# The FFN output matrix by the seven-product scheme for 12 of 22 depth tiles, with weight sums made partly by transfers

## The chip, the cores and the metric

One core of a Trainium2 chip runs the kernel. The metric is the device time of one execution in microseconds (us); the time before is the median of three timed runs.

## What is computed

One inference step of a hybrid streaming encoder with two layers, for 512 prompt tokens and 32 sample tokens of width 1024, all in 32-bit floats. Each layer has a SwiGLU feed-forward network (FFN) ahead of its mixer and one behind it, so there are four FFNs of inner width 2816:

```python
def swiglu(h, w_in, w_out):
    gate, up = jnp.split(h @ w_in, 2, axis=-1)
    return (jax.nn.silu(gate) * up) @ w_out

# per layer
x = x + 0.5 * swiglu(rms_norm(x, g1), w_in_a, w_out_a)
x = x + mixer(rms_norm(x, gm))
x = x + 0.5 * swiglu(rms_norm(x, g2), w_in_b, w_out_b)
```

The change touches the four FFNs, above all the product with `w_out` (2816 x 1024, that is 22 depth tiles of 128 by 1024 columns).

## The kernel before

The activations stand with their width on the 128 partitions and the 544 tokens along the free axis, two halves of 272 (`TH`). A product of 32-bit precision is made of three TensorE products: every operand is split into a high part (ScalarE copies it to `float32r`, L778 for weights) and a low part (VectorE subtracts, L784), and high x high, high x low and low x high are summed in PSUM.

An FFN is a list of units (`ffns`). For each of 11 column pairs of 256 columns there is a gate unit and an up unit of the input matrix. The first two pairs are plain (`LEAD_PAIRS`). The other nine go by Strassen's scheme in Winograd's form, here called seven-product: a 256 x 1024 block of weights is taken as 2 x 2 blocks, the tokens as 2 halves, and 7 products of half size take the place of 8 (`ffn_seven_pe`, L892, 7 x 4 x 3 = 84 matmuls of 272 columns). Four of its left factors are sums of weight blocks, which VectorE makes (`weight_sum_dve`, L1038 to L1046, buffers `wsum`), one unit ahead. The token sums stand in `bop`.

The output matrix is plain. Behind each of pairs 2 to 9 stands a `mid` unit (4 depth tiles by 512 columns, 96 matmuls, L793), and four `last` units take the last 6 tiles (72 matmuls each). The hidden rows of a pair are products in `sq`; ScalarE and VectorE split them into `hh` and `hl` (L951, L956).

The order is written out by hand, engine by engine. While TensorE runs product i of a unit, ScalarE and VectorE split product i of the next one, in a ring of 8 entries (`entry`, semaphores `op_hi`, `op_lo`, `op_used`). ScalarE also copies four of the seven products out of PSUM (`m1c`, `m5c`, `u2c`, `u3c`, L1155), and TensorE waits for a copy one product later. SP loads 1 MB of raw weights per unit into two slots (`raw`); a load waits until the unit two before it is split (`raw_free`). POOL has nothing to do in an FFN but its first microseconds and its end.

Of the kernel before, what the change touches and what calls it, by code (L numbers as in the profile page):

```python
# [29 lines left out]
P = 128  # L30
# [17 lines left out]
MID_TILES = 4  # L48
MID_PARTS = 4
LAST_TILES = FT - MID_TILES * MID_PARTS  # L50
RING = 8
# [104 lines left out]
def build(nc, ctx, io):  # L156
# [84 lines left out]
    ffn = Overlay(nc, arena.at, top)  # L241
    hh = ffn.buf("hh", [P, KT, T], F32R)
    hl = ffn.buf("hl", [P, KT, T], F32R)
# [5 lines left out]
    half_tiles = (KT // 2) * T * 4  # L249
    wsum_at = [Overlay(nc, arena.at + half_tiles, top), Overlay(nc, arena.at + 3 * half_tiles, top)]  # L250
    wsum_first = [w.buf(f"wsum_first{i}", [P, 4, KH, P]) for i, w in enumerate(wsum_at)]
    sum_at = Overlay(nc, norm_at.at, norm_end)
    wsum = [sum_at.buf(f"wsum{i}", [P, 4, KH, P]) for i in range(2)]
    comb_at = Overlay(nc, norm_at.at + KT * T * 4, norm_end)
    m1c, m5c, u2c, u3c = ([comb_at.buf(f"{name}{i}", [P, TH]) for i in range(2)] for name in ("m1c", "m5c", "u2c", "u3c"))
# [150 lines left out]
    sum_made = sig("sum_made")  # L406
    bank_copied = sig("bank_copied")
# [32 lines left out]
    comb = sig("comb")  # L440
# [106 lines left out]
    sm_tables = sig("sm_tables")  # L547
# [21 lines left out]
    def raw_index(u):  # L569

        return u + (0 if u < 1 else 33 if u < 20 else 66 if u < 21 else 99)
# [9 lines left out]
    sevens = []  # L581
    for f in range(4):
        units = []
        add = lambda kind, pair, s=0, part=0: units.append(Unit(f, len(units), kind, pair, s, part))
        for j in range(FJ):
            for s in range(2):
                add("whole" if j == 0 and s == 0 else "plain" if j < LEAD_PAIRS else "seven", j, s)
            if LEAD_PAIRS <= j < LEAD_PAIRS + 2 * MID_PARTS:
                add("mid", (j - LEAD_PAIRS) % 2, 0, (j - LEAD_PAIRS) // 2)
        for q in range(4):  # L590
            add("last", q, q % 2, MID_PARTS)
        ring_pos = (ring_pos + RING - 1) // RING * RING + KH
        for u in units:
            u.op = op_count
            u.n_ops = {"whole": 0, "plain": 4, "seven": 7, "mid": 4, "last": 4}[u.kind]
            if u.kind == "last":
                ring_pos += -ring_pos % 4
            if u.kind == "seven":
                u.seven = len(sevens)
                sevens.append(u)  # L600
            for i in range(u.n_ops):
                e = ring_pos % RING
                op_entry.append(e)
# [13 lines left out]
    first_seven = [u[2 * LEAD_PAIRS].seven for u in ffns]  # L617
    by_raw = {u.raw: u for units in ffns for u in units}
# [149 lines left out]
    def op_split_hi(act, u, i):  # L768
# [3 lines left out]
        if u.kind == "seven" and i in S_SUMS:  # L772
            act.wait_ge(sum_made.sem, sum_made.at(4 * u.seven + S_SUMS[i] + 1))
# [4 lines left out]
        nc.scalar.activation(entry(op)[0][:, 0:block_nk(u, i), :], op_source(u, i), ACT.Copy).then_inc(op_hi.sem, 1)  # L778
# [2826 lines left out]
```

## Time and profile before

| | us |
|---|---|
| timed runs, median (lowest, highest) | 2288.67 (2287.71, 2289.91) |
| profiled execution: its span from first to last instruction | 2285.9 |
| TensorE busy in it | 2249.8 (98%) |
| VectorE busy | 1633.5 (71%) |
| ScalarE busy | 1049.8 (46%) |
| POOL busy | 302.4 (13%) |

The profiled execution's own time is its span and the little that lies before its first and behind its last instruction; the timed runs are 1.8 to 4.0 us longer than the span. Shares of busy time are averages over the whole span. The granted clock of TensorE was 0.996 of 2.4 GHz in the mean.

### The profile page before, as it was taken

Reading aid. Unit: us, or ns where it says so; the run is one execution under the profiler, and the core shown is the slowest. Engines: PE = TensorE matmul, PEld = TensorE weight load, DVE = VectorE, ACT = ScalarE, POOL = GpSimd, SP = SyncE. Lnnn points to the kernel's source line nnn. Section 1 sums busy time; section 2 is a strip of 40 time slices with the busy share of each in tenths; the row PEclk is TensorE's granted clock in tenths of the full one; section 3 lists DMA queues with packets and bytes.
Section 4 is the critical chain, followed back from the end, with each engine's and each line's share of the span. In section 5 each row is a group of like instructions: output and inputs, shape, how many; then the busy total and the mean of one; then the engine's idle time right before and its main releaser. Section 6 shows DMA issues by size and latency. Waiting matters only on the chain.

```text
span 2285.9 us, 45730 instructions
## 1 busy us (share of the span) xinstructions
PE 2249.8 (98%) x18915; PEld 2198.7 (96%) x18915; DVE 1633.5 (71%) x2712; ACT 1049.8 (46%) x1949; POOL 302.4 (13%) x257
## 2 busy tenths in 40 slices
PE   9999999999999999999999999999999999999998
PEld 8999999988989999999999999999988899999998
DVE  7876776557575977767877776689755657777674
ACT  5544444333323544444554444454444544444443
POOL 2100002000051100001200000144033632000001
PEclk9999999999999999999999999999999999999999
DMA  4222323322202233222222232322310012222321
GB/s 135 93 93 97 103 92 110 98 81 83 90 10 93 75 101 103 93 93 93 93 93 93 96 105 87 114 74 75 93 52 2 30 31 91 93 93 93 98 97 68
DMA packets 175052, 194.82 MB, mean 85 GB/s; under 512 B 4826, under 2 KB 155870, under 8 KB 174841
## 3 DMA queue, kind: packets, MB, share of 16 engines
q1 hardware_dynamic: 161902, 181.64, 24.3%
q10 hardware_dynamic: 12306, 8.18, 1.3%
q8 instruction: 151, 2.47, 0.5%
q0 software_dynamic: 640, 2.10, 0.3%
q14 instruction: 53, 0.43, 0.1%
HBM read 185.80 MB, written 6.10 MB: 84 GB/s over the span
## 4 chain that ended last, share of the span: by engine, by line
PE 85%; DVE 8%; ACT 2%; issue 2%; POOL 1%; DMA 1%; ACTq 0%; SPq 0%; DVEq 0%; POOLq 0%
PE ps L892 33%; PE ps L793 29%; PE ps L666 12%; DVE cacc L2419 2%; DVE wl L651 1%; PE ps L3320 1%; DVE pre L2408 1%; ACT cacc L2488 1%; DMA xnat<-x_prompt 1%; PE ps L1681 1%; PE ps L3165 0%; POOL dBl L2996 0%; PE ps L2152 0%; PE ps L3150 0%; PE ps L3200 0%
## 5 line engine op out<-in xcount | busy, mean ns | idle before, releaser
L892 PE MATMUL ps<-bop,wh 128*128 128x272 f32 x4032 | 761.0, 288 | 0.0
L892 PEld LDWEIGHTS ps<-bop,wh 128*128 128x128 f32 x4032 | 633.0, 188 | 0.0
L892 PE MATMUL ps<-bop,wl 128*128 128x272 f32 x2016 | 582.2, 289 | 0.0
L784 DVE TENSOR_TENSOR wl<-raw,wh 128x512 fp32r<-128x512 f32 (+1 forms) x456 | 317.5, 708 | 266.8 <-ACT wh L778 262.1
L892 PEld LDWEIGHTS ps<-bop,wl 128*128 128x128 f32 x2016 | 378.8, 188 | 0.0
L778 ACT ACTIVATE wh<-raw 128x512 fp32r<-128x512 f32 (+1 forms) x456 | 265.3, 611 | 217.2 <-PE ps L793 177.4
L793 PE MATMUL ps<-hl,wh 128*128 128x288 f32 (+1 forms) x1408 | 290.4, 287 | 0.0
L793 PE MATMUL ps<-hh,wl 128*128 128x288 f32 (+1 forms) x1408 | 289.5, 287 | 0.0
L793 PE MATMUL ps<-hh,wh 128*128 128x288 f32 (+1 forms) x1408 | 289.1, 286 | 0.0
L666 PE MATMUL ps<-xh,wh 128*128 128x288 f32 (+1 forms) x1056 | 224.7, 294 | 2.1 <-DVE wl L651 2.1
L778 ACT ACTIVATE wh<-wsum 128x512 fp32r<-128x512 f32 x256 | 159.6, 627 | 132.8 <-DVE wsum L1038 86.6
L666 PE MATMUL ps<-xl,wh 128*128 128x288 f32 (+1 forms) x1056 | 217.9, 287 | 0.0
L666 PE MATMUL ps<-xh,wl 128*128 128x288 f32 (+1 forms) x1056 | 217.3, 287 | 0.0
L793 PEld LDWEIGHTS ps<-hh,wh 128*128 128x128 f32 x1408 | 215.8, 188 | 0.0
L793 PEld LDWEIGHTS ps<-hh,wl 128*128 128x128 f32 x1408 | 215.3, 188 | 0.0
L793 PEld LDWEIGHTS ps<-hl,wh 128*128 128x128 f32 x1408 | 215.0, 188 | 0.0
L784 DVE TENSOR_TENSOR wl<-wsum,wh 128x512 fp32r<-128x512 f32 x256 | 175.3, 686 | 17.4 <-ACT wh L778 14.0
L699 POOL COPY ssq<-sq 128x544 f32<-128x544 f32 x7 | 5.7, 810 | 1270.6 <-ACT sq L685 1270.6
L666 PEld LDWEIGHTS ps<-xh,wh 128*128 128x128 f32 x1056 | 161.6, 188 | 11.8 <-issue 7.4
L666 PEld LDWEIGHTS ps<-xl,wh 128*128 128x128 f32 x1056 | 161.5, 188 | 0.0
L666 PEld LDWEIGHTS ps<-xh,wl 128*128 128x128 f32 x1056 | 161.5, 188 | 0.0
L651 DVE TENSOR_TENSOR wl<-raw,wh 128x2048 fp32r<-128x2048 f32 x41 | 94.1, 2294 | 31.2 <-ACT wh L646 31.2
(490 smaller groups left out, 3586.5 us busy)
## 6 DMA issues: line engine op xcount, KB each, us to landing
raw<-ffn_w_in SPq DMA_DIRECT2D x88, 1024.0 KB, 5.0
raw<-ffn_w_out SPq DMA_DIRECT2D x32, 1024.0 KB, 5.1
raw<-odd_w_in SPq DMA_DIRECT2D x16, 1024.0 KB, 5.7
raw<-even_w_in SPq DMA_DIRECT2D x14, 1024.0 KB, 5.0
raw<-ffn_w_out SPq DMA_DIRECT2D x16, 768.0 KB, 4.2
raw<-even_w_out SPq DMA_DIRECT2D x4, 1024.0 KB, 5.0
raw<-odd_w_out SPq DMA_DIRECT2D x4, 1024.0 KB, 4.9
xnat<-x_prompt SPq DMA_DIRECT2D x2, 1024.0 KB, 11.9
```

Source lines behind the costliest of these rows:

```text
L651: nc.vector.tensor_tensor(wl[slot][:, 0:kt, :], raw[slot][:, 0:kt, :], wh[slot][:, 0:kt, :].bitcast(F32), ALU.subtract).then_inc(lo_done.s ...
L666: ins = nc.tensor.matmul(ps[:, 2 * pe_out + b, PCOLS[b]], w, r[:, rk, TOKENS[b]], start=first and a == 0, stop=last and a == 2)
L699: nc.gpsimd.tensor_copy(ssq[:], sq[0][:]).then_inc(ssq_done.sem, 1)
L778: nc.scalar.activation(entry(op)[0][:, 0:block_nk(u, i), :], op_source(u, i), ACT.Copy).then_inc(op_hi.sem, 1)
L784: nc.vector.tensor_tensor(lo[:, 0:nk, :], op_source(u, i), hi[:, 0:nk, :].bitcast(F32), ALU.subtract).then_inc(op_lo.sem, 1)
L793: ins = nc.tensor.matmul(ps[:, 2 * pe_out + b, PCOLS[b]], w[:, k, :], r[:, rk + k, TOKENS[b]], start=first and k == 0 and a == 0, stop=las ...
L892: ins = nc.tensor.matmul(ps[:, bank, 0:TH], w[:, k, :], bop[:, r, k, :], start=i in S_OPEN and k == 0 and a == 0, stop=k == KH - 1 and a = ...
L1681: ins = nc.tensor.matmul(ps[:, 4 + m, 0:width(b)], att[64 * m:64 * m + 64, h, b * P:(b + 1) * P], att[64 * m:64 * m + 64, 4 + h, 0:width(b ...
L2408: nc.vector.tensor_tensor(pre[c][:, 3:3 + SEQ], flat[:, PAT:PAT + SEQ], rstd[:, 0:SEQ], ALU.mult)
L2419: nc.vector.scalar_tensor_tensor(out=cacc[c][:], in0=pre[c][:, r:r + PADT - 3], scalar=cols[:, 7 * KT + 7 * i + r:7 * KT + 7 * i + r + 1], ...
L2488: nc.scalar.activation(cacc[i % 2][:], pre[i % 2][:, 0:PADT - 3], ACT.Copy, scale=cols[:, 7 * KT + 7 * i:7 * KT + 7 * i + 1]).then_inc(tap ...
L3320: ins = nc.tensor.matmul(ps[:, 2 * (2 * q + c) + b, OUT_COLS[b]], w, r[:, k, OUT_TOKENS[b]], start=k == 0 and a == 0, stop=k == KT - 1 and ...
```

## The change

Depth tiles 6 to 17 of the output matrix, two thirds (`part` 1 and 2) of 6 tiles each, go by the seven-product scheme: for each third four `out` units of 256 columns, 7 products of 3 tiles, 63 matmuls. Tiles 0 to 5 (`part` 0) stay plain, in four `mid` units of 72 matmuls, and tiles 18 to 21 in two `last` units of 96. The four units of a third stand between the gate and the up unit of pair 3, 6 and 9.

The right factors of the new products are the hidden rows. For pairs 3 to 8 VectorE makes four token differences of them (`hidden_turns`, into `hopf`), ScalarE and VectorE split seven blocks into `hop`, all in the gate unit of the next pair. Signs are turned so that all weight sums are additions (`minus`, `scale=-1.0`).

The two sums that are made of raw blocks alone (numbers 0 and 3) are no longer made by VectorE, other than in the first two input units of an FFN: POOL loads one block from DRAM into the buffer, waits, and adds the other with an accumulating transfer (`ffn_sums_pool`). Sums 1 and 2 stay with VectorE. The outcome of an `out` unit goes into `x` in five steps (`x_add`, `tail_dve`).

```diff
-MID_TILES = 4
-MID_PARTS = 4
+MID_PAIRS = 3
+MID_TILES = 2 * MID_PAIRS
+MID_PARTS = 3
...
         for j in range(FJ):
...
+            add("whole" if j == 0 else kind, j, 0)
+            if j and j % MID_PAIRS == 0:
+                for q in range(4):
+                    add("mid" if j == MID_PAIRS else "out", q, 0, j // MID_PAIRS - 1)
+            add(kind, j, 1)
+        for q in range(2):
+            add("last", q)
...
+    def sum_wait(eng, u, k):
+        if not early_block(u) and k in (0, 3):
+            eng.wait_ge(sum_added.sem, sum_added.at(32 * late_before(u) + 32))
...
+    def ffn_out_pe(pe, u):
...
+        for i, o in enumerate(S_ORDER):
...
+            elif i in (1, 5) and not first:
+                pe.wait_ge(x_part.sem, x_part.at(x_steps(u, 4) - X_STEPS))
+            elif i in (2, 3, 4):
+                pe.wait_ge(bank_copied.sem, bank_copied.at(4 * u.block + i - 1))
...
+            for k in range(MID_PAIRS):
+                for a, (w, r) in enumerate(((w_hi, 7 + o), (w_hi, o), (w_lo, 7 + o))):
+                    ins = nc.tensor.matmul(ps[:, block_bank(u, i), 0:TH], w[:, k, :], hop[k][:, r, :],
...
+    def hidden_turns(dve, u):
...
+        nc.vector.tensor_tensor(f[:, 3, :], sq[0][:, 0:TH], sq[0][:, TH:T], ALU.subtract).then_inc(turn_made.sem, 1)
+        nc.vector.scalar_tensor_tensor(out=f[:, 1, :], in0=sq[1][:, TH:T], scalar=-1.0, in1=sq[0][:, TH:T],
+                                       op0=ALU.mult, op1=ALU.subtract).then_inc(turn_made.sem, 1)
+        dve.wait_ge(turn_made.sem, turn_made.at(turns_before(u) + 1))
+        nc.vector.tensor_tensor(f[:, 2, :], sq[1][:, TH:T], f[:, 3, :], ALU.subtract).then_inc(turn_made.sem, 1)
+        dve.wait_ge(turn_made.sem, turn_made.at(turns_before(u) + 3))
+        nc.vector.tensor_tensor(f[:, 0, :], sq[1][:, 0:TH], f[:, 2, :], ALU.subtract).then_inc(turn_made.sem, 1)
...
+    def ffn_sums_pool(pool, f, w_in, w_out):
...
+        for u in ffns[f]:
+            if u.n_ops != 7 or early_block(u):
+                continue
+            out = sums_of(u)
+            if u.block - first_block[f] < 4:
+                pool.wait_ge(op_used.sem, op_used.at(ffns[f][3].op + 4))
+            else:
+                pool.wait_ge(op_lo.sem, op_lo.at(blocks[u.block - 2].op + 5))
+            pool.dma_start(out[:, 0, :, :], block(u, 1, 0)).then_inc(sum_loaded.sem, 16)
+            pool.dma_start(out[:, 3, :, :], block(u, 0, 0)).then_inc(sum_loaded.sem, 16)
+            pool.wait_ge(sum_loaded.sem, sum_loaded.at(32 * late_before(u) + 32))
+            pool.dma_start(out[:, 0, :, :], block(u, 1, 1), accum_op=ALU.add).then_inc(sum_added.sem, 16)
+            pool.dma_start(out[:, 3, :, :], block(u, 1, 0), accum_op=ALU.add).then_inc(sum_added.sem, 16)
...
+    def ffn_out_dve(dve, u):
+        v = ffns[u.f][u.at + 1]
+        weight_sum_dve(dve, v, 1)
+        next_split(dve, op_split_lo, u, 0)
+        tail_dve(dve, ffns[u.f][u.at - 1])
+        weight_sum_dve(dve, v, 2)
+        next_split(dve, op_split_lo, u, 1)
+        next_split(dve, op_split_lo, u, 2)
+        x_add(dve, u, 1)
+        next_split(dve, op_split_lo, u, 3)
+        x_add(dve, u, 2)
...
```

How it changes the order, at three places. In these rows a name behind the operation is output <- inputs, with its size, and in brackets the semaphores that the instruction waits for.

POOL in the first FFN, before: the gates of the lead, and then the sums of squares at the FFN's end.

```order
L1024 TENSOR_TENSOR gbuf_68<-gbuf_68,rstd 128x544 [waits gate_silu]
L1024 TENSOR_TENSOR gbuf_69<-gbuf_69,rstd 128x544 [waits gate_silu]
L699 COPY ssq<-sq 128x544 [waits sq_ready]
L703 TENSOR_TENSOR ssq<-ssq,sq 128x544 [waits sq_ready,ssq_done] x7
L1483 MEMSET qdec 128x64
```

POOL at the same place after (two blocks of the 24 of an FFN):

```order
L1185 TENSOR_TENSOR gbuf_69<-gbuf_69,rstd 128x544 [waits gate_silu]
L1229 DMA wsum_73<-ffn_w_in 128x4x128 [waits op_used]
L1230 DMA wsum_73<-ffn_w_in 128x4x128
L1232 DMA wsum_73<-ffn_w_in 128x4x128 [waits sum_loaded]
L1233 DMA wsum_73<-ffn_w_in 128x4x128
L1229 DMA wsum_72<-ffn_w_in 128x4x128 [waits op_lo]
L1230 DMA wsum_72<-ffn_w_in 128x4x128
L1232 DMA wsum_72<-ffn_w_in 128x4x128 [waits sum_loaded]
L1233 DMA wsum_72<-ffn_w_in 128x4x128
```

Four transfers per block stand there now, the third behind a wait for the landing of the first two.

VectorE just behind an up unit, before: the tail product, then sums and splits for the next unit, and the low parts of the hidden rows (`hl`) in a plain unit.

```order
L1206 TENSOR_TENSOR sq<-ps,gbuf_69 128x272 [waits block_silu,op_used]
L1038 TENSOR_TENSOR wsum_72<-raw 128x512 [waits raw_loaded1]
L784 TENSOR_TENSOR wl_50<-raw,wh_49 128x512 [waits op_hi]
L1041 TENSOR_TENSOR wsum_72<-wsum_72,raw 128x512 [waits sum_made]
L784 TENSOR_TENSOR wl_50<-wsum_72,wh_49 128x512 [waits op_hi]
L1216 SCALAR_TENSOR_TENSOR x<-ps,x 128x544 [waits x_part,op_used]
L1044 TENSOR_TENSOR wsum_72<-raw,wsum_72 128x512 [waits sum_made]
L1046 TENSOR_TENSOR wsum_72<-raw 128x512
L956 TENSOR_TENSOR hl<-sq,hh 128x544 [waits hh_ready]
```

VectorE at the same place after, in a gate unit:

```order
L1204 TENSOR_TENSOR wsum_73<-wsum_73,raw 128x512 [waits raw_loaded1,sum_added]
L1419 TENSOR_TENSOR sq<-ps,gbuf_69 128x272 [waits block_silu,op_used]
L1093 TENSOR_TENSOR hopf_79<-sq 128x272 [waits h_made]
L1094 SCALAR_TENSOR_TENSOR hopf_79<-sq 128x272
L1097 TENSOR_TENSOR hopf_79<-sq,hopf_79 128x272 [waits turn_made]
L1099 TENSOR_TENSOR hopf_79<-sq,hopf_79 128x272 [waits turn_made]
L824 TENSOR_TENSOR wl<-wsum_73,wh 128x512 [waits op_hi]
L1117 TENSOR_TENSOR hop_80<-sq,hop_80 128x272 [waits hh_ready]
L1207 TENSOR_TENSOR wsum_73<-raw,wsum_73 128x512 [waits sum_made]
L824 TENSOR_TENSOR wl<-wsum_73,wh 128x512 [waits op_hi]
L1114 SCALAR_TENSOR_TENSOR hop_80<-sq,hop_80 128x544 [waits hh_ready]
```

The first of them waits for POOL's transfers (`sum_added`); two of the four sums are gone, and the token differences and three low parts stand among the splits.

VectorE in an `out` unit, which was not there before:

```order
L1204 TENSOR_TENSOR wsum_73<-wsum_73,raw 128x384 [waits raw_loaded1,sum_added]
L824 TENSOR_TENSOR wl_50<-raw,wh_49 128x384 [waits op_hi]
L1424 SCALAR_TENSOR_TENSOR x<-ps,x 128x272 [waits x_part,op_used]
L1207 TENSOR_TENSOR wsum_73<-raw,wsum_73 128x384 [waits sum_made]
L824 TENSOR_TENSOR wl_50<-wsum_73,wh_49 128x384 [waits op_hi] x2
L1444 TENSOR_TENSOR x<-x,comb_74 128x272 [waits x_part,bank_copied]
L824 TENSOR_TENSOR wl<-wsum_73,wh 128x384 [waits op_hi]
L1448 TENSOR_TENSOR x<-x,comb_74 128x544 [waits x_part,bank_copied]
```

Here the splits are 384 columns wide, and the steps into `x` stand between them.

## Rows read from the trace of the kernel before

**Rows 1.** The page, busy time and the chain that ended last, by engine.

```profile
span 2285.9 us, 45730 instructions
PE 2249.8 (98%) x18915; PEld 2198.7 (96%) x18915; DVE 1633.5 (71%) x2712; ACT 1049.8 (46%) x1949; POOL 302.4 (13%) x257
...
PE 85%; DVE 8%; ACT 2%; issue 2%; POOL 1%; DMA 1%; ACTq 0%; SPq 0%; DVEq 0%; POOLq 0%
```

**Rows 2.** The chain in order of time, first FFN: start us, us, what.

```profile
106.14 21.12 PE ps L892 x168
127.26 12.01 PE ps L793 x96
139.27 21.11 PE ps L892 x168
160.38 11.96 PE ps L793 x96
...
193.44 11.91 PE ps L793 x96
...
337.62 21.09 PE ps L892 x168
358.71 35.87 PE ps L793 x288
394.58 6.02 PE ps L666 x48
```

**Rows 3.** Busy time by stage, first FFN; the last two columns are DMA share and GB/s.

```profile
core 0: us, PE busy (x) PEld busy (x) DVE busy (x) ACT busy (x) POOL busy (x), PEclk, DMA share, GB/s
94.16:106.14 11.98, 11.98 (x99) 11.98 (x98) 11.98 (x22) 4.65 (x8) 0.00 (x0) 1.00 0.28 89
127.26:139.27 12.01, 12.01 (x99) 12.01 (x98) 11.33 (x19) 4.76 (x8) 0.00 (x0) 1.00 0.29 91
139.27:160.38 21.11, 21.11 (x171) 21.11 (x170) 12.58 (x23) 10.91 (x23) 0.00 (x0) 1.00 0.29 100
```

**Rows 4.** VectorE in order of time: start us, us, line, operation, tiles, sizes.

```profile
58.94 1.27 DVE L972 TENSOR_TENSOR bop<-bopf,bop 128x1088 fp32r<-128x1088 f32 x1
60.14 0.67 DVE L1041 TENSOR_TENSOR wsum_first<-wsum_first,raw 128x512 f32<-128x512 f32 x1
...
127.13 0.72 DVE L1259 TENSOR_TENSOR sq<-sq,gbuf 128x544 f32<-128x544 f32 x1
127.77 0.43 DVE L1206 TENSOR_TENSOR sq<-ps,gbuf 128x272 f32<-128x272 f32 x1
128.12 0.68 DVE L1038 TENSOR_TENSOR wsum<-raw 128x512 f32<-128x512 f32 x1
128.72 0.69 DVE L784 TENSOR_TENSOR wl<-raw,wh 128x512 fp32r<-128x512 f32 x1
...
146.08 0.69 DVE L784 TENSOR_TENSOR wl<-wsum,wh 128x512 fp32r<-128x512 f32 x1 [0.21 <-ACT wh L778]
...
149.02 0.69 DVE L784 TENSOR_TENSOR wl<-raw,wh 128x512 fp32r<-128x512 f32 x1 [0.18 <-ACT wh L778]
```

**Rows 5.** ScalarE in order of time, in an up unit.

```profile
154.39 0.40 ACT L1155 ACTIVATE u2c<-ps 128x272 f32<-128x272 f32 x1 [1.11 <-PE ps L892]
154.68 0.62 ACT L778 ACTIVATE wh<-raw 128x512 fp32r<-128x512 f32 x1
...
157.71 1.67 ACT L778 ACTIVATE wh<-raw 128x512 fp32r<-128x512 f32 x3
```

**Rows 6.** Transfers in 139.27:160.38, then 440:450, then 466:474: packets, MB, share of 16 engines.

```profile
q1 hardware_dynamic: 1560, 2.08, 28.4%
...
raw<-ffn_w_in SPq DMA_DIRECT2D x1, 1024.0 KB, 4.8
...
q10 hardware_dynamic: 676, 0.32, 15.5%
q0 software_dynamic: 80, 0.26, 7.5%
...
q0 software_dynamic: 80, 0.26, 12.3%
```

**Rows 7.** POOL's loads of 256 KB, tiles pks and pvs: issue ns, landing us.

```profile
L1487 POOL DMA_DIRECT2D pks<-cache_attn_k x4: 747/748/919, 398.4 to 515.7; - x4
DMA to landing us min/median/max: 3.8/5.5/6.5
...
L1490 POOL DMA_DIRECT2D pvs<-cache_attn_v x4: 747/748/757, 399.4 to 544.1; - x4
...
DMA to landing us min/median/max: 3.2/3.5/3.9
```

**Rows 8.** SP's issues of raw loads in order of time.

```profile
138.02 0.37 SPq L1447 DMA_DIRECT2D raw<-ffn_w_out  x1
149.74 11.02 SPq L1447 DMA_DIRECT2D raw<-ffn_w_in  x2
```

**Rows 9.** A group of instructions by line: POOL's sums of squares (busy us, mean ns).

```profile
L703 POOL TENSOR_TENSOR ssq<-ssq,sq 128x544 f32<-128x544 f32 x49 | 70.5, 1439 | 125.1 <-ACT sq L685 123.6 <-POOL ssq L703 1.1 <-POOL ssq L699 0.4
```

More of the change, by code:

```diff
@@ L585, in build @@
         for j in range(FJ):
[L586 to L591, printed above, removed]
+            kind = "plain" if j < LEAD_PAIRS else "seven"
+            add("whole" if j == 0 else kind, j, 0)
[5 more added lines that the diff above has]
+            add("last", q)
         ring_pos = (ring_pos + RING - 1) // RING * RING + KH
@@ L594, in build @@
             u.op = op_count
-            u.n_ops = {"whole": 0, "plain": 4, "seven": 7, "mid": 4, "last": 4}[u.kind]
+            u.n_ops = {"whole": 0, "plain": 4, "seven": 7, "out": 7, "mid": 4, "last": 4}[u.kind]
             if u.kind == "last":
-                ring_pos += -ring_pos % 4
+                ring_pos += -ring_pos % (RING if u.pair == 0 else 4)
             if u.kind == "seven":
@@ L600, in build @@
                 sevens.append(u)
+            if u.kind == "out":
+                u.out = len(outs)
+                outs.append(u)
+            if u.n_ops == 7:
+                u.block = len(blocks)
+                blocks.append(u)
             for i in range(u.n_ops):
                 e = ring_pos % RING
+                if u.kind == "last" and u.pair == 0:
+                    e = (i + 2) % 4
                 op_entry.append(e)
@@ new lines, in x_steps, with x_before, hidden_before @@
+    def x_steps(u, step):
+        if u.kind == "mid":
+            return X_LAYER * u.f + 2 * u.pair + step
+        return X_LAYER * u.f + 8 + X_STEPS * (4 * (u.part - 1) + u.pair) + step
+    def x_before(u, step):
+        if u.part == 1:
+            return X_LAYER * u.f + 2 * u.pair + 2
+        return x_steps(u, step) - 4 * X_STEPS
+    def hidden_before(f, pair):
+        whole = MID_PAIRS * MID_PARTS
+        done = lambda j: 2 * j + min(max(j - MID_PAIRS, 0), whole - MID_PAIRS)
+        return f * done(FJ) + done(pair)
@@ L1187, in ffn_last_act @@
             split_hi(act, next_unit, 0)
-        for c in range(2):
-            feed_act(act, n, 2 * u.pair + c, c, not final)
+        for c in range(4):
+            feed_act(act, n, 4 * u.pair + c, c % 2, not final)
     def ffn_act(act, f, n, next_unit=None):
@@ L1311, in ffn_last_dve @@
                 feed_dve(dve, n, m)
+        if q == 0:
+            tail_dve(dve, before)
+            op_split_lo(dve, u, 2)
+            op_split_lo(dve, u, 3)
+            hidden_lo(dve, before, 0)
+            hidden_lo(dve, before, 1)
+            for i in range(4):
+                op_split_lo(dve, ffns[f][u.at + 1], i)
+        for m in range(4 * q, 4 * q + 4):
+            update(m)
+            if m == 4 and next_unit is not None:
+                split_lo(dve, next_unit, 0)
+            if m:
+                feed(m - 1)
+        if q:
+            feed(KT - 1)
     def ffn_dve(dve, f, n, next_unit=None):
```

533 lines of the change are left out of this document (339 added, 194 removed).

## The prediction

> **What bounds the kernel now.** I read the chain that ended last, first by engine [rows 1]: TensorE holds 85% of it, VectorE 8%. Then the same chain in order of time through the first FFN [rows 2]. The reader is to see that each piece begins where the one before ended: 106.14 + 21.12 is 127.26, 127.26 + 12.01 is 139.27, and so on to 394.58. A piece of L892 with 168 matmuls is a pair of seven-product units, a piece of L793 with 96 a plain unit of the output matrix, the one with 288 the four last units. No wait stands between them, and the other three FFNs look the same. Third, busy time by stage [rows 3]: TensorE is full everywhere, VectorE has 12.58 us of work in the 21.11 us of a pair and 11.33 in the 12.01 of a plain output unit, the DMA engines are 0.29 busy. So in an FFN a matmul less is a matmul's time less, as long as VectorE, ScalarE and the transfers keep up. What the change is worth is first a count of matmuls and then a question to those three.
>
> **TensorE.** A pair of units takes 21.09 to 21.12 us for 168 matmuls [rows 2], 0.1256 us each. The eight plain units of an FFN take 11.91 to 12.01 [rows 2], 11.97 in the mean, 0.1247 per matmul; the 288 of the last units 35.87, 0.1245. Before, the output matrix of one FFN has 8 x 96 + 288 = 1056 matmuls: 95.7 + 35.9 = 131.6 us. After: four plain units of 72 (6 tiles, 2 column halves, 3 products, 2 token halves), 288 x 0.1247 = 35.9; eight seven-product units of 63 (7 products, 3 tiles, 3), 504 x 0.1256 = 63.3; two last units of 96, 192 x 0.1245 = 23.9; sum 123.1. That is 8.5 us less per FFN and **34 us less** in four. The 18 seven-product input units of an FFN, 84 matmuls each, are not touched.
>
> **VectorE.** Its instructions overlap at their ends, so I count starts [rows 4]: 0.60 us for 512 columns (128.12 to 128.72), 0.64 for 544, 0.35 for 272, 1.20 for 1088 (58.94 to 60.14); 384 columns, interpolated, 0.47. In a gate unit behind an up unit of pairs 3 to 8 it now has 7 low parts (4.2), 2 weight sums (1.2), the tail product (0.35), 4 token differences (1.4), low parts of 272, 544 and 1088 columns (2.2) and 3 sums (1.05): 10.4 of 10.55 us. The up unit has 4.2 + 1.2 + 5 small ones 2.0 = 7.4. An output unit of 7.91 has 7 x 0.47 + 2 x 0.47 + 3 x 0.35 + 2 x 0.64 = 6.6; the fourth, which splits for a 512-column unit, 7.7. Three pairs and four output units make 79.9 us of 95.0, 84%, where it was 72% [rows 3]. Before, VectorE was busy 11.98 of 11.98 us in the first plain unit and TensorE did not wait [rows 3]: the splits run seven products ahead, so a lag of a microsecond in the gate unit is caught up in the up unit. I cost VectorE at nothing. If that cover fails, below. ScalarE has 7 splits, 4 copies and the new high parts, 7 x 0.56 + 4 x 0.30 + 1.9 = 7.0 of 10.55 in the gate unit [rows 5]; its copy has to be done one product (1.51 us, in output units 1.13) after it may start and takes 0.40, so it too has cover.
>
> **Transfers.** Of the four sums of 64 input units and all 32 output units, two leave VectorE: per block POOL now issues two loads of 256 KB, waits for both, issues two accumulating ones, and ScalarE waits for these before it splits product 1. In a 21.11 us pair the two raw loads hold the 16 engines for 28.4%, 6.0 us, so 3.0 per MB [rows 6]. A 256 KB load from POOL in the same 512-byte pieces held them 12.3% of 8 us, 0.98, or 7.5% of 10 us, 0.75 [rows 6]. No row shows an accumulating transfer. A gain is excluded, since it moves what a load moves and reads its destination too; so its lower end is 0.75. The dearest 512-byte row is the ScalarE queue's stores, 15.5% of 10 us for 0.32 MB [rows 6], 1.27 for 256 KB; read twice that is 2.5, my upper end. I take 1.6, two quiet loads, nearer the lower end since the sizes and the queue are those of the POOL rows. A unit then needs 3.0 + 2 x 0.98 + 2 x 1.6 = 8.2 of its 10.55 us of engine time (10.0 at the upper end), an output unit three quarters of that, 6.1 (7.5) of 7.91. So it fits at both ends, narrowly at the upper one.
>
> The Trainium skill, in "Collectives: The Full Stack", section "The bandwidth ceiling: the fold count and why AG ≠ RS ≠ AR", says that an add in the transfer costs no cycles of its own but two source reads, so that a reducing transfer ran at half the rate of a copy. No run here shows that yet; by it an accumulate is two of the 0.98, an estimate of 2.0 us, and the unit needs 9.0 of 10.55, the same verdict.
>
> **The wait that is added.** What counts is also how long the four transfers take one behind the other. POOL issues in 0.75 us, a load lands 3.2 to 6.5 us after its issue [rows 7]. Two steps of issue and landing are 7.9 us at the quick end, 14.5 at the slow one, plus at most 2 x (2.5 - 0.75) = 3.5 for the adding. The buffer comes free when VectorE has the fifth low part of the block before last, 7.5 us into a unit (146.08 + 0.69 - 139.27 [rows 4]) or, in the fuller gate unit, about 9.7. The sums are wanted about 3.3 us into the unit after next, since ScalarE must split product 1 and copy the second product before TensorE's fourth at 4.5. That leaves 14.7 us (0.85 + 10.55 + 3.3) or 16.6 for input units; for output units and the one or two behind them 1.7 + 7.9 + 2.4 = 12.0. Queued behind a late sum are ScalarE's copies, for which TensorE waits, and VectorE's next sum. I take landings of 3.8 and 1.7 for the adding: 10.8 us, which is 4 us early in input units and 1 us early at the ends of the output groups. With some late ones there, I put 2 us on the whole kernel (eight groups, a quarter of a microsecond each). At the slow end, 18 against 14.7 and 12.0 and halved because two blocks are in flight, it would be 106 us for the 64 input units alone.
>
> **Raw loads.** The next load starts when the seventh low part is done (149.02 + 0.69; SP issues at 149.74 [rows 4, 8]) and takes 4.8 [rows 6]. It now shares the engines with 5.2 us of the POOL queue's work in the same unit: 10.0 at worst, of 9.4 to 10.7 and some 2 us until TensorE's third product feels it. Nothing, or half a microsecond in some units. I add 0.5 us in all.
>
> **Ends of the FFNs.** The chunks of 1/8 of the output now end every 24 matmuls, 3.0 us, instead of 36. What follows each of them, VectorE's update (0.64) and low part, ScalarE's high part and square and POOL's sum of squares at 1.44 [rows 9], is under 3 us on each engine, and POOL's last weight sum is issued more than a unit before. I cost it at nothing; a microsecond either way per FFN lies inside the range.
>
> **Sum.** The profiled execution has a span of 2285.9 us; the three timed runs stand 1.8 to 4.0 above it, the median 2.8. 2285.9 - 34 + 2.5 = 2254.4 of span, with 2.8 around it **2257**.
>
> **Rivals.**
> (a) **The accumulating transfers are slow** and the transfers become the bound, by engine time or, with landings at the slow end, by the chain above. It decides where 3.0 + 1.96 + 2A passes 10.55, at A = 2.8 us per 256 KB. At A = 3.5 a unit needs 12.0 and an output unit 9.0: 64 x 1.4 + 32 x 1.1 = 125 us, less 34 and more 2.8 around: 2285.9 + 91 + 2.8 = 2380, slower. For it: 512-byte pieces, two thirds of the engine time already spoken for, no row of its own kind, two landings in series with the slowest seen at 6.5 [rows 7]. Against: the POOL queue's pieces are the cheapest per byte in the trace [rows 6].
> (b) **VectorE becomes the bound** in the gate units. The last two token differences each wait for the one before, as do other pairs; at 0.2 us for five such waits the gate unit has 11.4 us for 10.55. If the up unit doesn't give it back, 24 gate units cost 0.85 each, 20 us: 2275, still faster. Against it speak the full VectorE of the first plain unit [rows 3] and 3 us of room in each up unit.
> (c) **Most of it is given back** by late sums around the output groups and raw loads that land late in them: 1 us in each of 32 output units gives 2287, no difference.
>
> **How the numbers follow.** My forecast, 2251 to 2265: 0.58. (b) or a part of (c), 2265 to 2284: 0.13. (c) in full, 2284 to 2293: 0.06. (a): 0.23, spread from 2293 up with a long tail, since each half microsecond of A past its point costs 64 x 1.0 + 32 x 0.75 = 88 us. A measurement of this kernel can tell 0.2%, 4.6 us, from no change: faster 0.71, same 0.06, slower 0.23. The first three cases hold 0.77; with the near end of (a) up to 2300 the range 2250 to 2300 holds 0.8.
>
> **What would show it.** In the profile after, the chain in time should show output groups of 252 matmuls in about 31.7 us and last units of 192 in 23.9, and 288 matmuls fewer. Right: TensorE full in every FFN stage, sums landing before ScalarE wants them, VectorE near 84%. Wrong by (a): ScalarE's splits of wsum waiting for DMA, pairs longer than 21.1 us, the DMA share near 1. Wrong by (b): VectorE full in gate units and TensorE waiting for wl. Wrong by (c): waits in and just behind output groups alone.

## The result, and the profile after

The changed kernel takes 2360.42 us (median of 4 runs, 2357.14 to 2370.72) against 2288.19 us: **3.2% slower**, a ratio of 1.032 with an interval of 1.031 to 1.034. The forecast was 2257 us, faster. The profiled execution has a span of 2354.9 us, 69.0 more than before.

The page of the kernel after, busy time, the transfer queues (packets, MB, share of 16 engines) and the chain by engine and line, to be read against [rows 1]:

```profile
span 2354.9 us, 46614 instructions
PE 2245.2 (95%) x18627; PEld 2187.7 (93%) x18627; DVE 1705.3 (72%) x2960; ACT 1166.3 (50%) x2229; POOL 707.5 (30%) x641
...
q0 software_dynamic: 108160, 94.40, 23.0%
...
PE 65%; DMA 15%; DVE 9%; POOL 5%; issue 4%; ACT 2%; ACTq 0%; SPq 0%; DVEq 0%; POOLq 0%
```

The 288 matmuls are gone (18915 to 18627). But TensorE holds 65% of the chain instead of 85%, and transfers and POOL, 2% together before, now hold 20%.

The chain in order of time through the first output group, to be read against [rows 2], where no wait stood between the pieces:

```profile
106.28 36.07 PE ps L1000 x288
142.35 52.79 PE ps L932 x420
...
203.99 0.77 POOL wsum L1229
204.75 4.84 DMA wsum<-ffn_w_out
209.89 1.29 POOL wsum L1232
211.18 1.32 POOL wsum L1233
212.50 0.62 POOL wsum L1229
213.11 5.99 DMA wsum<-ffn_w_out
219.40 1.29 POOL wsum L1232
220.68 1.31 POOL wsum L1233
221.99 0.79 POOL wsum L1229
222.78 2.87 issue
225.65 6.59 DMA wsum<-ffn_w_in
232.53 0.77 POOL wsum L1232
233.31 7.47 DMA wsum<-ffn_w_in
241.86 6.06 PE ps L979 x36
```

The plain output units take 36.07 us, as costed, and five units of 84 matmuls follow without a gap. From 203.99 to 240.78 the path runs through POOL and its transfers alone: two loads (L1229, L1230), their landing, two adding issues (L1232, L1233), and only then the loads of the next block. (240.78 is 233.31 + 7.47, where the last landing ends.) What the chain releases is in ScalarE's order of time (what ended the idle time stands in brackets):

```profile
232.44 0.38 ACT L1356 ACTIVATE comb<-ps 128x272 f32<-128x272 f32 x1
240.80 0.63 ACT L818 ACTIVATE wh<-wsum 128x512 fp32r<-128x512 f32 x1 [7.99 <-DMA wsum<-ffn_w_in]
241.34 0.38 ACT L1356 ACTIVATE comb<-ps 128x272 f32<-128x272 f32 x1
```

ScalarE stands 7.99 us in front of a late sum, and behind it in ScalarE's order is a copy of a product (`comb`) that TensorE waits for. So a late sum of the *next* unit stops TensorE in *this* one. Over the whole span (us, times, longest):

```profile
DVE wsum L1204 <- DMA wsum<-ffn_w_in: 72.7, 23, 9.3
ACT wh L818 <- DMA wsum<-ffn_w_in: 65.9, 22, 8.7
DVE wsum L1204 <- DMA wsum<-ffn_w_out: 59.6, 20, 7.4
PE ps L979 <- ACT comb L1356: 55.6, 15, 7.9
```

By place, in windows of the first FFN (the columns of [rows 3]; an output group is 252 matmuls):

```profile
142.18:205.50 63.32, 63.32 (x507) 63.32 (x505) 55.78 (x104) 40.12 (x81) 24.93 (x24) 1.00 0.81 182
205.50:247.76 42.26, 33.62 (x255) 33.05 (x253) 26.66 (x54) 20.84 (x47) 16.18 (x17) 0.92 0.76 173
247.76:312.58 64.82, 63.77 (x506) 63.39 (x505) 55.49 (x104) 40.01 (x81) 24.64 (x24) 1.00 0.79 180
312.58:353.58 41.00, 34.18 (x254) 33.80 (x253) 27.37 (x56) 20.96 (x47) 14.38 (x16) 0.92 0.72 168
353.58:393.36 39.78, 33.18 (x255) 32.99 (x253) 20.89 (x39) 17.18 (x35) 5.83 (x6) 0.91 0.50 119
```

A group takes 41 to 42 us here (38.8 to 44.4 in all four FFNs) where the prediction said 31.7. Of the first group's 10.7 us too many, 8.6 are idle time; in the other 2.1 TensorE is busy for 33.62 us with what takes 31.54 at full clock, at a granted clock of 0.92 of 2.4 GHz in the mean of that stretch. The mean is made of two levels. TensorE stood idle from 234.5 to 241.86 us, and around the end of that wait the clock is 0.50, that is 1.2 GHz:

```profile
237.95:244.78 6.83, 2.92 (x13) 2.95 (x14) 3.98 (x8) 2.79 (x6) 2.15 (x2) 0.50 0.58 121
```

The 36 matmuls behind the wait take 6.06 us (last row of the chain above), 1.6 more than 36 take in 31.54 us for 252. In the full stretches the clock is 1.00.

### The profile page after: what moved, and what is told of

Read it like the earlier page. It is cut to its first block, busy times and chain, and to the rows that moved or that the text cites. A ratio compares the mean times of both kernels' runs of the same rounds, so it can differ in the third digit from the quotient of the medians.

```text
span 2354.9 us, 46614 instructions
## 1 busy us (share of the span) xinstructions
PE 2245.2 (95%) x18627; PEld 2187.7 (93%) x18627; DVE 1705.3 (72%) x2960; ACT 1166.3 (50%) x2229; POOL 707.5 (30%) x641
## 3 DMA queue, kind: packets, MB, share of 16 engines
q0 software_dynamic: 108160, 94.40, 23.0%
## 4 chain that ended last, share of the span: by engine, by line
PE 65%; DMA 15%; DVE 9%; POOL 5%; issue 4%; ACT 2%; ACTq 0%; SPq 0%; DVEq 0%; POOLq 0%
PE ps L932 22%; PE ps L688 15%; DMA wsum<-ffn_w_in 9%; PE ps L833 8%; PE ps L1000 6%; DMA wsum<-ffn_w_out 5%; PE ps L1034 2%; POOL wsum L1232 2%; PE ps L979 1%; POOL wsum L1233 1%; PE ps L3577 1%; DVE wl L673 1%; DVE cacc L2676 1%; POOL wsum L1229 1%; DVE wl L824 1%
## 5 line engine op out<-in xcount | busy, mean ns | idle before, releaser
L824 DVE TENSOR_TENSOR wl<-raw,wh 128x512 fp32r<-128x512 f32 (+1 forms) x456 | 291.9, 657 | 57.5 <-ACT wh L818 52.7
L979 PE MATMUL ps<-hop,wh 128*128 128x272 f32 x1344 | 269.7, 300 | 55.9 <-ACT comb L1356 55.6
L818 ACT ACTIVATE wh<-wsum 128x512 fp32r<-128x512 f32 (+1 forms) x384 | 226.4, 590 | 183.8 <-DMA wsum<-ffn_w_in 65.9
L824 DVE TENSOR_TENSOR wl<-wsum,wh 128x512 fp32r<-128x512 f32 (+1 forms) x384 | 243.8, 642 | 49.4 <-ACT wh L818 47.7
L979 PEld LDWEIGHTS ps<-hop,wh 128*128 128x128 f32 x1344 | 223.0, 199 | 59.8 <-issue 59.7
L1356 ACT ACTIVATE comb<-ps 128x272 f32<-128x272 f32 x416 | 163.8, 394 | 187.3 <-PE ps L932 146.9
L979 PE MATMUL ps<-hop,wl 128*128 128x272 f32 x672 | 199.9, 297 | 0.0
L1232 POOL DMA_DIRECT2D wsum<-ffn_w_in x64 | 83.8, 1310 | 306.4 <-DMA wsum<-ffn_w_in 306.4
L688 PEld LDWEIGHTS ps<-xh,wh 128*128 128x128 f32 x1056 | 162.2, 189 | 12.7 <-issue 7.9
L1204 DVE TENSOR_TENSOR wsum<-wsum,raw 128x512 f32<-128x512 f32 (+1 forms) x96 | 61.8, 643 | 132.7 <-DMA wsum<-ffn_w_in 72.7
L1229 POOL DMA_DIRECT2D wsum<-ffn_w_in x64 | 72.1, 1127 | 247.4 <-DVE wl L824 219.5
L979 PEld LDWEIGHTS ps<-hop,wl 128*128 128x128 f32 x672 | 133.5, 199 | 0.0
```

Of the source, the lines that this page charges most:

```text
L688: ins = nc.tensor.matmul(ps[:, 2 * pe_out + b, PCOLS[b]], w, r[:, rk, TOKENS[b]], start=first and a == 0, stop=last and a == 2)
L818: nc.scalar.activation(entry(op)[0][:, 0:block_nk(u), :], op_source(u, i), ACT.Copy).then_inc(op_hi.sem, 1)
L824: nc.vector.tensor_tensor(lo[:, 0:nk, :], op_source(u, i), hi[:, 0:nk, :].bitcast(F32), ALU.subtract).then_inc(op_lo.sem, 1)
L979: ins = nc.tensor.matmul(ps[:, block_bank(u, i), 0:TH], w[:, k, :], hop[k][:, r, :], start=i in S_OPEN and k == 0 and a == 0, stop=k == MI ...
L1204: nc.vector.tensor_tensor(out[:, 1, :, :], out[:, 0, :, :], block_raw(u, 0, 0), ALU.add).then_inc(sum_made.sem, 1)
L1229: pool.dma_start(out[:, 0, :, :], block(u, 1, 0)).then_inc(sum_loaded.sem, 16)
```

## Experiments

All times are medians beside runs of the kernel before on the same chip (2288.3 to 2288.8 us). Stage times come from each kernel's own trace. Two words are used throughout: the *chain* of a block is the time from the issue of its first load to the landing of its last adding transfer, and its *window* the time from that first load to ScalarE's first split of a sum of that block, when nothing is late.

### Which blocks lose: half of them by transfers

in_only leaves transfers to the 64 input blocks, out_only to the 32 output blocks; VectorE makes the other sums, as it does in early blocks.

```diff
+    def by_dma(u):
+        return not early_block(u) and u.kind != "out"     # out_only: == "out"
...
-            if u.n_ops != 7 or early_block(u):
+            if u.n_ops != 7 or not by_dma(u):
```

> Output units make all four weight sums on VectorE again; only the 64 input blocks keep POOL's transfers. Theory 1 (the late sums come from POOL's serial chain, which takes 8.4 to 8.7 us and more per block from one first load to the next where an output unit has 7.91, so it falls behind inside the output groups and delivers late until behind them): the 75.7 us that the eight output groups lose go, with most of the 22 us in the input units between and behind them; groups of 252 matmuls near 31.7 us, 2265 to 2280 in all. Theory 2 (the engines' time for the adding is the limit): the input blocks still move 1 MB by transfers per unit, so pairs of input units keep losing; 2290 to 2320. Theory 3 (VectorE is too full): its work per output unit rises from about 6.6 to 7.5 of 7.91 us, the groups stay above 34 us; over 2300.

> The converse: all input units make their four sums on VectorE, only the 32 output blocks go by transfers. Theory 1 in the form of occupancy and backlog: POOL comes to each group idle and the first two blocks' sums are early; it then falls behind by 0.5 to 0.8 us per block, so a group loses 1 to 3 us instead of 10; about 2275 to 2290. Theory 1 in the form of latency (12.3 us of chain against a window of 12.0, whatever stands ahead): the groups still lose 5 us or more each; 2300 to 2340. Theory 3: gate units hold about 11.6 us of VectorE work in 10.55; pairs rise above 21.2 us each, 20 us more in 24 pairs.

in_only: 2318.43 us, ratio 1.0135 (1.012 to 1.015). The groups come down to 31.5 to 33.7 us, but the input units between and behind them now lose: their three-pair stretches behind a group take 65.0 to 71.5 us instead of 63.3, the last stretch of three units of each FFN 33.4 to 43.1 instead of 31.7. The 2265 to 2280 of theory 1 was wrong: the blocks right behind a group are as exposed as those in it. The time lies in the range of theory 2 (2290 to 2320), so the places have to decide. Three windows of its first FFN, ahead of the first group, behind it and behind the second:

```profile
141.44:204.75 63.31, 63.31 (x506) 63.31 (x505) 55.77 (x104) 40.26 (x81) 15.17 (x14) 1.00 0.67 157
236.99:301.99 65.00, 63.79 (x507) 63.41 (x506) 57.44 (x108) 40.28 (x81) 16.76 (x16) 1.00 0.68 159
333.50:373.72 40.22, 34.04 (x254) 33.65 (x253) 21.73 (x41) 17.17 (x35) 4.65 (x5) 0.92 0.50 118
```

Ahead of a group every unit moves its 1 MB too, at the same share of the engines (0.67), and nothing is lost; by theory 2 it should be. out_only: 2314.35 (four runs from 2303 to 2320), ratio 1.011 (1.008 to 1.014); nearly all its loss lies in the groups, 36.2 to 41.9 us each. That is the latency form of theory 1; the idle queue at the group's start did not help. Theory 3 fails in both: in_only's groups stay below 34 us, and in out_only VectorE's fuller units run at 63.5 us per three pairs.

### No transfers, and transfers that don't add

dve_all is the same edit with `by_dma` always false. no_add keeps every wait:

```diff
-            pool.dma_start(out[:, 0, :, :], block(u, 1, 1), accum_op=ALU.add).then_inc(sum_added.sem, 16)
-            pool.dma_start(out[:, 3, :, :], block(u, 1, 0), accum_op=ALU.add).then_inc(sum_added.sem, 16)
+            pool.dma_start(out[:, 0, :, :], block(u, 1, 1)).then_inc(sum_added.sem, 16)
+            pool.dma_start(out[:, 3, :, :], block(u, 1, 0)).then_inc(sum_added.sem, 16)
```

> No sum goes by transfers: VectorE makes all four in every seven-product unit, the new output units included. VectorE then has about 20.2 of 21.1 us in a pair with hidden splits and 7.5 of 7.91 in an output unit. Theory 1 and 2: all of the loss goes, the matmul count alone is left, 2255 to 2265. Theory 3 (VectorE becomes the bound when it is 95% full): 2275 to 2300, with TensorE waiting for wl in the gate units.

> The two accumulating transfers of each block become plain loads of the same blocks to the same place, with the same waits (the blocks' sums 0 and 3 are then not added up, and the outcome is wrong by that part). It takes the adding away and leaves the chain of two issues and two landings. If the adding itself is the cost (2.08 against some 0.98 us of engine time for 256 KB, and issues of 1.3 and 1.9 us against 0.8): the groups fall to about 32 us and the kernel to 2265 or less. If two landings in series on one queue are the cost: per block the chain gets shorter by about 1.5 us of issue and some landing, 11 against 12.3 us, the groups stay at 34 to 38 us and the kernel at 2290 to 2330.

dve_all: **2258.56 us**, ratio 0.987 (0.985 to 0.989), faster than both kernels. Three pairs and a group of it:

```profile
141.45:204.98 63.53, 63.53 (x507) 63.42 (x506) 60.42 (x113) 40.67 (x81) 0.00 (x0) 1.00 0.28 92
204.98:236.52 31.54, 31.54 (x255) 31.54 (x253) 30.86 (x63) 20.98 (x47) 0.00 (x0) 1.00 0.36 118
```

VectorE is busy 95% and 98% of these stretches and TensorE does not wait: the room that the transfers were to make was not needed. no_add: 2258.75, ratio 0.987 (0.986 to 0.989). The same chain of two issues, a landing, two issues and a landing, over the same bytes, costs next to nothing when the second pair is plain. The queue on its page, and POOL's two second issues in input units among the groups by line (busy us, mean ns of one):

```profile
q0 software_dynamic: 29312, 94.40, 14.2%
...
L1233 POOL DMA_DIRECT2D wsum<-ffn_w_in x64 | 47.9, 748 | 0.5 <-issue 0.5
L1232 POOL DMA_DIRECT2D wsum<-ffn_w_in x64 | 47.9, 748 | 232.9 <-DMA wsum<-ffn_w_in 224.9 <-issue 8.0
```

The same two groups in the changed kernel:

```profile
L1233 POOL DMA_DIRECT2D wsum<-ffn_w_in x64 | 118.7, 1855 | 0.0
L1232 POOL DMA_DIRECT2D wsum<-ffn_w_in x64 | 83.8, 1310 | 306.4 <-DMA wsum<-ffn_w_in 306.4
```

The adding ones take 1.31 and 1.86 us instead of 0.75 each; they overlap, and POOL is free 2.6 us after the start of the first (209.89 to 212.50 in the chain above) instead of 1.5. From issue of the first load to the last landing a block takes, in the median, 9.0 us (output) and 10.9 us (input) in no_add, 12.3 and 13.4 in the changed kernel.

### Half a dose, and the same dose issued late

one_sum leaves only sum 0 to transfers: one load and one adding transfer per block.

```diff
-        elif k == 3 and early:
+        elif k == 3:
...
-            pool.dma_start(out[:, 3, :, :], block(u, 0, 0)).then_inc(sum_loaded.sem, 16)
...
-            pool.dma_start(out[:, 3, :, :], block(u, 1, 0), accum_op=ALU.add).then_inc(sum_added.sem, 16)
```

one_late is one_sum with the load of a block issued later.

```diff
-                pool.wait_ge(op_lo.sem, op_lo.at(blocks[u.block - 2].op + 5))
+                pool.wait_ge(op_lo.sem, op_lo.at(blocks[u.block - 1].op + 2))
```

Theory A in the expectations from here on is that loads standing in POOL's one queue behind the adding transfers of the block before make the next block late; theory B, that the adding itself costs, wherever the loads stand.

> Half a dose: per block only sum 0 goes by transfers (one load, one accumulating), sum 3 is made by VectorE. POOL's work per block falls from about 8.5 to 6 us (0.78 + 3.5 + 1.3), the chain from 12.3 to about 9 us (one landing of 3.5, one of 4.3, issues). Theory A and the reading by chain and window both expect no late sums: 2258 to 2265. Theory B by engine time halves the loss: 2300. If VectorE's third sum costs anything, dve_all with four sums has already shown that it does not.

> one_sum (one load and one accumulating transfer per block), but issued later: when VectorE has the second low part of the block directly before, instead of the fifth of the block before last, 4.5 us later in output units and some 6 us later in input units. The same transfers, the same engine time, less than half of the accumulating ones of the changed kernel. By chain and window the blocks then stand one behind the other: a unit lasts at least the chain plus about 1.5 us of splits, 8.0 + 1.5 = 9.5 against 7.91 in output units and 9.4 + 1.5 = 10.9 against 10.55 in input units; 32 x 1.6 + 64 x 0.4 = 77 us, about 2330. By engine time or slow adding as such: no change from one_sum, 2255 to 2260.

one_sum: **2255.19 us**, ratio 0.986 (0.984 to 0.987), the lowest median here, though its interval overlaps that of dve_all. Its chain in order of time is what the prediction had drawn:

```profile
104.89 36.07 PE ps L1000 x288
140.97 63.32 PE ps L932 x504
204.28 31.54 PE ps L979 x252
235.82 63.31 PE ps L932 x504
299.13 31.51 PE ps L979 x252
```

Without stalls its trace also shows the real window: 12.8 to 15.2 us in steady input units, 12.7 to 14.4 in the first two output units, but 10.5 us in the third and fourth output unit and 10.9 to 11.4 in the two blocks behind them. ScalarE is there a little before TensorE needs it (in sp_loads2, below, a wait of 2.1 us there left TensorE idle for 1.4). The chains of one_sum (8.0 us output, 9.4 input) fit.

one_late: 2458.11, ratio 1.074 (1.073 to 1.076), with the same transfers. POOL in the first group:

```profile
211.62 0.77 POOL L1229 DMA_DIRECT2D wsum<-ffn_w_out  x1 [5.74 <-DVE wl L824]
215.04 1.28 POOL L1231 DMA_DIRECT2D wsum<-ffn_w_out  x1 [2.64 <-DMA wsum<-ffn_w_out]
224.74 0.77 POOL L1229 DMA_DIRECT2D wsum<-ffn_w_out  x1 [8.43 <-DVE wl L824]
```

The blocks stand one behind the other, 13.1 us from load to load where a unit has 7.91, and groups take 47 to 51 us. That latency against a window decides, at a light load on the transfer engines, is shown. The size was off (about 2330 expected): the chain grew to 10 us in the group, and from landing to VectorE's second low part it is 3.1 us, not 1.5.

### The same work, issued earlier or on another queue

early_load changes one wait: slot 0 of the buffer is loaded three products earlier.

```diff
-                pool.wait_ge(op_lo.sem, op_lo.at(blocks[u.block - 2].op + 5))
+                pool.wait_ge(op_lo.sem, op_lo.at(blocks[u.block - 2].op + 2))
             pool.dma_start(out[:, 0, :, :], block(u, 1, 0)).then_inc(sum_loaded.sem, 16)
+            if u.block - first_block[f] >= 4:
+                pool.wait_ge(op_lo.sem, op_lo.at(blocks[u.block - 2].op + 5))
```

> The changed kernel with the same four transfers per block, but the load of sum 0 no longer waits for the whole buffer: it is issued when VectorE has the second low part of the block before last (slot 0 of the buffer is not read after that), three products earlier; the load of sum 3 keeps its wait. Nothing is taken away, so a theory that the adding costs engine time or slows other transfers expects no change, 2350 to 2365. The theory that the sums come late because two loads, two landings and two adding issues stand in series after the buffer is free expects from the load of sum 3 on 0.8 + 3.3 + 6.2 = 10.3 us in output blocks and about 11 in input blocks, where the copy without stalls (one_sum) leaves 10.5 us in the third and fourth output unit and 11.0 to 11.4 in the two blocks behind: most of the 100 us of stalls goes, 2262 to 2285.

2314.68 us, ratio 1.012 (1.010 to 1.014): 46 us better than the changed kernel, 30 short of what was expected. Five of its eight groups take 31.8 to 32.8 us, among them both of the third FFN, in windows:

```profile
1298.86:1331.19 32.33, 31.78 (x255) 31.59 (x253) 26.10 (x52) 20.87 (x47) 15.93 (x15) 1.00 0.90 214
...
1395.56:1427.88 32.32, 31.75 (x254) 31.56 (x253) 26.07 (x52) 20.92 (x47) 15.91 (x15) 1.00 0.91 213
```

The changed kernel's two groups in that FFN:

```profile
1321.60:1360.40 38.80, 34.22 (x254) 33.93 (x253) 25.63 (x52) 20.91 (x47) 15.15 (x15) 0.91 0.80 183
1424.26:1468.70 44.44, 34.41 (x254) 33.85 (x253) 27.16 (x55) 20.84 (x47) 16.99 (x17) 0.88 0.73 168
```

With the same transfers the engines are busy 0.90 of the time and TensorE loses 0.8 us per group; in the changed kernel they are busy 0.73 to 0.80 and it loses 7 to 13. So the engines' time is not what stops it. The other three groups, the first ones of FFNs 1, 2 and 4 (39.8 to 41.5 us), and the last seven-product units of FFNs 1, 2 and 4 (36.3 to 40.3, where one_sum has 31.7) hold most of what is left. At just those places POOL stands still between two issues. The changed kernel's POOL at the first of them, in order of time:

```profile
220.16 1.83 POOL L1233 DMA_DIRECT2D wsum<-ffn_w_out  x1
221.06 1.72 POOL L1229 DMA_DIRECT2D wsum<-ffn_w_in  x1
225.65 0.77 POOL L1230 DMA_DIRECT2D wsum<-ffn_w_in  x1 [2.87 <-issue]
```

It has nine such stalls, 32.6 us of idle time, always at the second load of the 12th, 17th and 23rd of an FFN's 24 blocks (none in the third FFN), and each ends 0.25 us after the last adding transfer of the block before has landed. Where that one has landed in time, as always in one_sum, there is none. In early_load the same issues of the same FFNs go out 0.25 us after the landing.

sp_loads gives the two plain loads to SP's hardware queue, and sp_loads2 places the first two blocks' loads better.

```diff
-            pool.dma_start(out[:, 0, :, :], block(u, 1, 0)).then_inc(sum_loaded.sem, 16)
-            pool.dma_start(out[:, 3, :, :], block(u, 0, 0)).then_inc(sum_loaded.sem, 16)
             pool.wait_ge(sum_loaded.sem, sum_loaded.at(32 * late_before(u) + 32))
+            pool.wait_ge(sum_added.sem, sum_added.at(32 * late_before(u)))
...
+        sp.dma_start(out[:, 0, :, :], sum_block(u, 1, 0, wi, wo)).then_inc(sum_loaded.sem, 16)
+        sp.dma_start(out[:, 3, :, :], sum_block(u, 0, 0, wi, wo)).then_inc(sum_loaded.sem, 16)
```

> The two plain loads of each block are issued by SP on its hardware queue (ahead of the raw load of the same unit, behind the same wait for the buffer), POOL is left with the wait for them and the two accumulating transfers (behind the landing of the block before). The adding stays as dear as it is. Theory A (queue: what costs is that loads stand in POOL's one queue behind the accumulating transfers of the block before, land after 5.5 to 9 us instead of 3.5, and make the next block late in turn): loads land in about 3.5 to 4.5 us, the chain falls from 12.3 to about 10.5 us in output blocks, the groups to 32 to 33 us, 2262 to 2275 in all. Theory B (the adding itself, by its engine time and its 3.2 us of issue and 4.3 to 6 us of landing, wherever the loads stand): the groups still lose 3 to 8 us each, 2290 to 2330. SP also waits for buffers now, with the raw loads queued behind it: if that is late, TensorE waits for raw in up units.

> As sp_loads, but the loads of the first two late blocks of an FFN stand together behind the raw load of the first of them; in sp_loads the second pair stood behind the raw loads of the plain output units and came 40 us late, so that the plain output units took 41 to 42 us instead of 36.1. Expected by chain and window: these 20 us go; the output blocks (10.2 us of chain) are in time, the first input block behind a group (13.7 us of chain against 11.0) stays late by 2 to 3 us; 2290 to 2300. If the loads' place on POOL's queue were the whole cause: 2262 to 2275.

sp_loads: 2322.81 (ratio 1.014), in the range of theory B; sp_loads2: 2307.47 (1.008, 1.005 to 1.010), 7 us above what was expected. In sp_loads2 the output blocks' chain is 10.1 us and the groups take 32.4 to 35.9 us, so that all eight lose 16.6 us together where the changed kernel loses 76.8; ScalarE still waits about 2 us for the input blocks behind them, whose chain is 13 to 16 us against the 11. The first three seven-product units of each FFN take 36.7 to 38.9 us instead of 31.6, a loss that the expectation did not have: the first block's loads are issued at 76.3 us instead of 73.6 and its adding transfers take up to 8.3 us to land. So loads that stand in line behind adding transfers are a good part of the groups' loss, and not the whole cause: with the loads on another queue the chain of the input blocks behind a group is still longer than their window.

### The sums on POOL itself

In pool_add the four transfers of a block go, and POOL adds out of the raw slots:

```diff
+            nc.gpsimd.tensor_tensor(out[:, 0, :, :], block_raw(u, 1, 0), block_raw(u, 1, 1), ALU.add).then_inc(sum_added.sem, 1)
+            nc.gpsimd.tensor_tensor(out[:, 3, :, :], block_raw(u, 0, 0), block_raw(u, 1, 0), ALU.add).then_inc(sum_added.sem, 1)
```

> POOL makes sums 0 and 3 itself, by two additions of 512 or 384 columns out of the raw slots, with the same wait for the buffer and one for the raw load; no transfers for sums. By POOL's rows (1.38 us for 512 columns) that is 2.8 us of POOL per unit of 10.55 and 2.1 per output unit of 7.91, and the raw block lands a unit ahead, so sums come early. If engines do not disturb each other: as dve_all or 1 to 2 us less, 2255 to 2259. If POOL's additions slow VectorE's instructions (both read the same buffers): VectorE's splits of 512 columns rise from 0.69 us, 2260 to 2275.

2294.86 us, ratio 1.003 (1.002 to 1.004), 20 us above the dearer of the two expectations. VectorE's splits of sums, 686 ns in one_sum, take 801, and three pairs of units (second row, a window) last 66.02 us with VectorE busy 62.19 of them:

```profile
L824 DVE TENSOR_TENSOR wl<-wsum,wh 128x512 fp32r<-128x512 f32 x256 | 203.7, 801 | 17.2 <-ACT wh L818 14.2
...
141.34:207.36 66.02, 64.48 (x507) 63.55 (x505) 62.19 (x98) 39.78 (x81) 17.57 (x12) 1.00 0.27 89
```

The transfers are gone, and VectorE is slower while POOL adds: of those 256 splits the 183 that no addition of POOL overlaps take 0.68 us in the mean, the 39 that lie beside one for over four fifths of their length 1.36. ScalarE waits 58.7 us in all for the sum of L1207, 30.0 at the same place of dve_all. That VectorE is the bound here is read from these rows; VectorE was as busy in dve_all (95%) without holding anything up, and no further run tested it.

## Why the prediction was wrong

**TensorE: right.** Plain units 36.07 us for 288 matmuls (35.9 costed), groups 31.5 (31.7), last units 23.9 (23.9). Where nothing stalls, in one_sum, the span is 2253.0, 32.9 below before; 34 were costed, and 2254.4 was the span forecast.

**VectorE at nothing: right,** with more to spare than I claimed. Three pairs and a group were costed at 79.9 us of 95.0, 84% (the terms add up to 80.9); they hold 82.4 in the changed kernel (55.78 and 26.66 in the windows above), and in dve_all VectorE is busy 95% without harm. Rival (b) did not decide; pool_add is the run nearest to it.

**Transfers by engine time: right in the verdict, wrong in a reason.** The queue's share of 16 engines rose from 14.2% of 2255.1 us in no_add to 23.0% of 2354.9 for the same 94.40 MB: 221 us more, for 46.1 MB of adding transfers, 1.26 us per 256 KB. A plain one there is 0.89 (313 us, without 7 for the other loads, for 92.3 MB), so an adding one is 2.15, inside my 0.75 to 2.5 but above the 1.6 taken. I put it near the low end because "the sizes" were those of the POOL rows. They were not: 80 packets for 0.26 MB stand in [rows 6], 3.3 KB each, and the adding transfers bring 78,848 more packets, as 46.1 MB in pieces of 512 bytes do against 4 KB. The Trainium skill ("Collectives: The Full Stack", section "The bandwidth ceiling: the fold count and why AG ≠ RS ≠ AR") says a reducing transfer reads two sources and runs at half a copy's rate; here it is 2.4 times a copy's engine time, and the measurement stands. Neither figure decides the result. (In rival (a) "two thirds of the engine time already spoken for" is under a half by the prediction's own terms, 3.0 + 1.96 of 10.55 us.)

**"The wait that is added" is the step that failed:** 2 us on the whole kernel, 101.9 measured (2354.9 less 2253.0): 76.8 in the eight groups, 24.5 in seven-product input units. Three of its numbers were off. The chain was taken as 10.8 us and is 12.3 in output and 13.4 in input blocks in the median, up to 20.8. Issue was taken as 0.75 us; adding ones take 1.31 and 1.86, and the second load of a block starts 0.8 us after the first and lands about 1 us later still. And the windows, 12.0 and 14.7 by my sum, are 10.5 to 11.4 and 12.8 to 15.2 in one_sum. (The 16.6 beside them is 16.9 by its own terms, and was not used.)

**What I left out** is that POOL is one queue. A block's loads cannot be issued before the adding transfers of the block before, and these wait for a landing. In the first group POOL starts blocks at 203.99, 212.35 and 221.06, 8.4 to 8.7 us apart, where an output unit has 7.91. I took two blocks in flight as halving a late chain; they pass through POOL one at a time, and a block that starts late finds its loads behind adding transfers, so lateness feeds itself. Loads that were issued while adding transfers of the block before were under way land after 4.7 us in the median and up to 10.6; those of one_sum, where no block is late, after 3.1 (output) and 3.4 (input). It is rival (a), which had 0.23, by its chain and not by engine time, at the places that I gave to rival (c), and at three times the 32 us that (c) had. I gave (a) by the chain the slow landings everywhere as its condition; three or four late blocks in and just behind each group were enough.

**The clock.** I costed a wait at its length. The matmuls behind it took more time too: a group's 252 took up to 34.6 us of busy time instead of 31.5, at a mean granted clock of 0.88 to 0.92 (2.4 GHz with stretches at 1.2).

**Raw loads: too low, without effect.** Their median landing rose from 5.0 to 6.8 us; what TensorE waited for in the groups was ScalarE's copies, which stood behind late sums.

## What to carry to other kernels

Before work is moved off an engine, ask whether the engine was in the way: at 95% busy VectorE still held nothing up, and the transfers that relieved it put a serial chain with a deadline in its place. Cost such a chain by its issuing queue as well as its latency (the time from one block's first issue to the next block's against the shortest unit) and read the deadline where units are shortest. Look also at what stands behind a wait in the order of the engine that waits: ScalarE's wait for the next unit's sum stopped TensorE in this unit, and of the 10.7 us that the first group lost, 1.6 went to the 36 matmuls behind the wait, at the lower clock.

## What was not expected of the hardware

- An adding transfer from POOL's queue went in 512-byte packets, 108,160 packets where plain loads of the same bytes made 29,312; it held the engines for 2.15 us per 256 KB against 0.89, and POOL's issue for 1.31 to 1.86 us against 0.75.
- POOL stopped for up to 6.1 us between two issues, until an earlier adding transfer had landed. Why at these places is open. They seem to follow what the queue has been given: from the 12th to the 17th and from there to the 23rd block POOL issues 5.0 MB each time, and other runs move them. In in_only POOL stops at the 11th and 16th of an FFN's 16 blocks in FFNs 1 and 2 and at the 5th, 10th and 15th in the third, again five blocks of 1 MB apart; in sp_loads2, with only the adding transfers on POOL, before the second of them in the 17th block (FFNs 1 and 2, up to 5.7 us).
- Two additions of 512 columns per unit on POOL (1.6 us each) slowed VectorE's subtractions from 0.69 to 0.80 us in the mean, from 0.68 to 1.36 where they lay beside one.
- What was not separated: how much of an adding transfer's price lies in its issue and how much in its landing. Both lengthen the same chain.
